# Up projections of the MLP: each 512-column product paired at once with its 256-column product, in place of eight and then eight

## The chip, the cores and the metric

The kernel runs on one core of a Trainium2 chip. The time of a run is the device time of that core in microseconds (us). The kernel before took 2586.78 us (median of three runs, 2585.1 to 2587.87).

## The reference

The program computes two layers of a hybrid encoder trunk over 256 tokens of width 2048, all in float32. Layer 0 has a Mamba-2 mixer, layer 1 an MLA attention mixer; each layer then has a squared-ReLU MLP and a gated per-layer input. The change touches the first product of the MLP, `hn @ w1`:

```python
D_MODEL = 2048; SEQ = 256; DEPTH = 2; D_FF = 4 * D_MODEL

def sq_relu_mlp(hn, w1, w2):
    return jnp.square(jax.nn.relu(hn @ w1)) @ w2

def reference(x, p, ...):
    h = x
    for i in range(DEPTH):
        hn = rmsnorm(h, ln_mix[i])
        h = h + (mamba2_mixer(hn, ...) if i < N_A else mla_mixer(hn, ...))
        h = h + sq_relu_mlp(rmsnorm(h, ln_mlp[i]), mlp_w1[i], mlp_w2[i])
        h = per_layer_input(h, p[i], ple_norm[i], ple_gate_w[i], ple_proj_w[i])
    return h
```

So for each of the two layers the up projection multiplies 256 x 2048 activations by a 2048 x 8192 matrix.

## The kernel before

Every float32 operand of a large matrix product is split into a high part and a rest ("hi" and "lo"), and the product is the sum hi x hi + hi x lo + lo x hi. Weights come from memory in slices of 2 x 128 rows by 512 columns (512 KB), through eight buffers `raw`. For each slice the scalar engine writes the high part to `w_hi` (line 647) and the vector engine the rest to `w_lo` (line 1197). Both have four slots, picked by `g % SPL`, where `g` counts slices. The semaphore "lo" says that a slice's rest is written; the semaphore "used", raised by the last product of a slice, gives its slot back to the scalar engine, which waits for it before it converts the slice four places further on.

TensorE works through the slices in a fixed order written in the program. Most projections are a `unit`: eight slices, each of 24 products of 512 columns (lines 1842 to 1844, in `half_chunk`), where the activations are the stationary operand and the weights stream.

The up projection, `up` inside `mlp`, is the other way round: the weights are stationary, in blocks of 128 x 128, and the activations stream. For one slice (this text calls that a round) there are four groups of output features (`f`) and two row tiles of the slice (`k`), which makes eight blocks. The high activations and their rest lie side by side in `xa_both`, 256 columns each, so that one product of 512 columns with a block of `w_hi` gives hi x hi in the first half of a bank of PSUM and hi x lo in the second (line 2083). A product of 256 columns with the block of `w_lo` then adds lo x hi into the first half (line 2089). Each `f` has a bank of its own (two in each of two pairs; the pairs are "acc_a" or "acc_b", "mid" and "tp" in the profile). Before, a round does the eight products of 512 columns for all four banks, then the eight of 256 columns. Every product has its own weight load just ahead of it.

Each `up(j)` is eight rounds, one for each slice of the 2048 rows, and each layer has 16 of them: four `up` in a row, 32 rounds, then units of the down projection. This makes 8 blocks of 32 rounds, 256 rounds in all. Between the first rounds of a layer's first block, jobs (`turn_h`) put eight transposes of `h` between two rounds: twice in layer 0 and once in layer 1. The round starts with a wait for "lo" (line 2076), and `hold` waits until a pair of banks has been read out, before the first product into it.

Of the kernel before, what the change touches and what calls it, by code (L numbers as in the profile page):

```python
# [105 lines left out]
def trunk_kernel(nc, x, p, positions, ln_mix, ln_mlp, mlp_w1, mlp_w2, ple_norm, ple_gate_w, ple_proj_w,  # L106
# [4 lines left out]
    with ctx:  # L111
# [36 lines left out]
        def part(*shape):  # L148
# [7 lines left out]
            if len(shape) == 3:  # L156
# [57 lines left out]
        halves = {"A": acc_a[:, :, :], "B": acc_b[:, :, :], "M": mid_both[:, :, :],  # L214
                  "T": tflat.rearrange("p (b n) -> p b n", b=2)}
# [1599 lines left out]
        def _(pe):  # L1815
            w = Walk(pe)

            def hold(banks, event):

                for b in banks:  # L1820
                    if b in w.busy:
                        name, k = w.busy[b]
                        pe.wait_ge(S[name], w.at(name, k))
                k = w.tick(event) + 1
                for b in banks:
                    w.busy[b] = event, k
# [22 lines left out]
            def chunk(*args):  # L1849

                for _ in half_chunk(*args):
                    pass
# [21 lines left out]
            def unit(x, pair, event, jobs=None, need=None):  # L1874


                hold(pair, event)
                for n in range(8):
                    if need and n % 2 == 0:
                        pe.wait_ge(S["act"], w.at("act", need[n // 2]))  # L1880
                    chunk(x, 2 * n, pair, n == 0, n == 7)
                    for job in (jobs or {}).get(n, ()):
                        job()

            def flip(src, per, n, m):

                for j in range(n):
                    for t in range(m):
                        last = pe.transpose(per(j, t), src(j, t), ident[:, :])  # L1889
                return last  # L1890
# [9 lines left out]
            def turn_h(blk, updates, scaled=True):  # L1900

                def job():
                    if updates:
                        pe.wait_ge(S["hadd"], updates)
                    if scaled:
                        hold_scaled()
                    else:
                        hold("T", "act")
                    flip(lambda j, t: h[:, t, 512 * blk + P * j:512 * blk + P * j + P], feature, 4, NT)\
                        .then_inc(S["Th"], 1)  # L1910
                return job
# [154 lines left out]
            def needs(posted):  # L2066

                return [w.k["act"] - posted + 1 + n for n in range(4)]

            def mlp(layer, pp, turns, posted):  # L2070
                def up(j, jobs=None, need=None):
                    for n in range(8):
                        if need and n % 2 == 0:
                            pe.wait_ge(S["act"], need[n // 2])
                        g = w.tick("G")
                        pe.wait_ge(S["lo"], g + 1)
                        for f in range(4):
                            half = (pp[0] + "M", "T" + pp[1])[j % 2][f // 2]
                            if n == 0 and f % 2 == 0:
                                hold(half, "u")  # L2080
                            dst = halves[half][:, f % 2]
                            for k in range(2):
                                pe.matmul(dst, w_hi[:, g % SPL, k, P * f:P * f + P],  # L2083
                                          xa_both[:, 2 * n + k].rearrange("p a t -> p (a t)"),
                                          start=n == 0 and k == 0, stop=False)
                        for f in range(4):
                            dst = halves[(pp[0] + "M", "T" + pp[1])[j % 2][f // 2]][:, f % 2]
                            for k in range(2):
                                mm = pe.matmul(dst[:, 0:TOK], w_lo[:, g % SPL, k, P * f:P * f + P],  # L2089
                                               xa_both[:, 2 * n + k, 0], start=False, stop=n == 7 and k == 1)  # L2090
                        mm.then_inc(S["used"], 1)
                        for job in (jobs or {}).get(n, ()):
                            job()

                def turn_p():
                    pe.wait_ge(S["pin"], 16 * (layer + 1))
                    hold("T", "act")
                    flip(lambda j, t: p_sb[:, t, P * j:P * j + P], feature, 2, NT).then_inc(S["Tp"], 1)

                base = 32 + 32 * layer + 12  # L2100
                up(0, turns, needs(posted))
                for q in range(4):
                    for j in range(1, 4):
                        up(j)
                    done = w.k["act"]
                    w.skip("act", 4)
                    unit(ya, pp[0], "hadd", None, range(done + 1, done + 5))
                    if q < 3:
                        for j in range(1, 4):
                            unit(ya, pp[j % 2], "hadd")  # L2110
                        up(0)
                unit(ya, pp[1], "hadd", {1: [turn_h(0, base + 1)]})
                unit(ya, pp[0], "hadd", {1: [turn_h(1, base + 2)], 4: [turn_p]})
                unit(ya, pp[1], "hadd", {1: [turn_h(2, base + 3)]})
                c = w.k["act"]
                pe.wait_ge(S["act"], c - 1)
                for n, pair in enumerate((pp[0], "M", pp[1], "M")):
                    hold(pair, "pj")
                    chunk(pt, 0, pair, True, True)
                    if n == 1:  # L2120
                        turn_h(3, base + 4)()
                jobs = lambda n, slot: {slot: [turn_h(n, base + 5 + n, scaled=False)]} if layer == 0 else {}
                unit(xa, pp[0], "gs", None, [c - 3, c - 2, c, c + 1])
                for n in range(2 + (layer == 0)):
                    unit(xa, pp[(n + 1) % 2], "gs", jobs(n, 3))
                if layer:
                    hold(pp[1], "gs")
                    for n in range(6):
                        chunk(xa, 2 * n, pp[1], n == 0, False)
                    g = w.k["G"]  # L2130
                    pe.wait_ge(S["lo"], g + 2)
                    for t, a, b in LAST_PIECES:
                        rows, dst = slice(t * P, t * P + P), acc[pp[1]][t][:, a:b]
                        for k in range(4):
                            xh, xl = xa[0][:, 12 + k, rows], xa[1][:, 12 + k, rows]
                            slot = (g + k // 2) % SPL
                            wh, wl = w_hi[:, slot, k % 2, a:b], w_lo[:, slot, k % 2, a:b]
                            pe.matmul(dst, xh, wh, start=False, stop=False)
                            pe.matmul(dst, xh, wl, start=False, stop=False)
                            mm = pe.matmul(dst, xl, wh, start=False, stop=k == 3)  # L2140
                        mm.then_inc(S["fin"], 1)
                w.skip("hadd", NB)
                return base
# [192 lines left out]
```

## Time and profile before

| | |
|---|---|
| runs before, median (lowest to highest) | 2586.78 us (2585.1 to 2587.87) |
| the profiled execution's own time | 2585.33 us |
| its span, first to last instruction | 2583.5 us |
| TensorE products busy | 2568.7 us, 99% of the span |
| TensorE weight loads busy | 2174.3 us, 84% |
| vector engine busy | 1657.0 us, 64% |
| scalar engine busy | 1262.2 us, 49% |
| GpSimd busy | 103.2 us, 4% |
| data read from memory | 486.38 MB, 189 GB/s over the span |
| granted TensorE clock | 1.000 of full speed |

All rows come from one profiled execution; its time lies 2585.33 - 2583.5 = 1.83 us over its span, for what comes before the first and after the last instruction. Products follow one another in a pipeline: the recorded duration of one (390 ns for one of 512 columns) is longer than the distance to the start of the next, so the cost of a product is read from the distance between starts in the list of instructions by time, not from its duration. In that list the first column is the start in us from the span's start, the second the time until the last instruction of the row ends, then the engine, line, operation, the output and inputs, and how many equal instructions one row stands for. "PE" are products, "PEld" weight loads. A product of 512 columns reads "128x512", one of 256 columns "128x256"; "128*128" is the block of weights (rows by columns).

### The profile page before, as it was taken

The numbers are of one execution on the slowest core, as the hardware profiler recorded it, in microseconds if no ns is written. First come the engines' busy times: TensorE is split into PE (matmuls) and PEld (weight loads), VectorE is DVE, ScalarE is ACT, GpSimd is POOL, SyncE is SP. The second block draws the span as 40 slices with busy tenths as digits, with TensorE's granted clock in tenths as the row PEclk, the third lists the DMA queues.
The fourth block names the chain that finished last, engine by engine and source line by source line (L and its number), as shares of the span: only waits on it lengthen the run. The fifth ranks groups of instructions, "written<-read, shape, count | busy, mean of one in ns | idle before, by whom it ended". The sixth has DMA issues, their size and how long they took to land.

```text
span 2583.5 us, 31623 instructions
## 1 busy us (share of the span) xinstructions
PE 2568.7 (99%) x12792; PEld 2174.3 (84%) x12792; DVE 1657.0 (64%) x1881; ACT 1262.2 (49%) x1528; POOL 103.2 (4%) x214
## 2 busy tenths in 40 slices
PE   9999999999999999999999999999999999999999
PEld 8888888888888888888888888888888888888887
DVE  6678888888755565555555567767655555555655
ACT  6545555555544443443445557655434434434453
POOL 2000000000000000000000002100000000000000
PEclk9999999999999999999999999999999999999999
DMA  7587887876565655656655554446556566566553
GB/s 258 156 280 242 235 240 240 240 224 203 175 193 194 189 190 193 189 193 193 190 192 180 189 170 134 144 157 180 190 192 189 193 193 189 189 194 188 192 187 130
DMA packets 263665, 503.11 MB, mean 195 GB/s; under 512 B 21840, under 2 KB 27208, under 8 KB 263520
## 3 DMA queue, kind: packets, MB, share of 16 engines
q1 hardware_dynamic: 259344, 490.88, 60.1%
q0 software_dynamic: 2656, 8.58, 1.2%
q8 instruction: 101, 1.65, 0.3%
q10 hardware_dynamic: 1520, 1.64, 0.2%
q14 instruction: 44, 0.36, 0.0%
HBM read 486.38 MB, written 2.16 MB: 189 GB/s over the span
## 4 chain that ended last, share of the span: by engine, by line
PE 95%; DVE 2%; DMA 1%; ACT 1%; issue 0%; POOL 0%; SPq 0%; ACTq 0%; DVEq 0%
PE acc_b L1842 10%; PE acc_b L1844 10%; PE acc_b L1843 10%; PE acc_a L1842 10%; PE acc_a L1844 10%; PE acc_a L1843 10%; PE tp L2083 5%; PE acc_b L2083 5%; PE acc_a L2083 5%; PE mid L2083 5%; PE mid L2089 2%; PE acc_b L2089 2%; PE acc_a L2089 2%; PE tp L2089 2%; PE tp L1889 2%; PE mid L2022 1%
## 5 line engine op out<-in xcount | busy, mean ns | idle before, releaser
L1197 DVE TENSOR_TENSOR w_lo<-raw,w_hi 128x1024 fp32r<-128x1024 f32 x874 | 1060.9, 1220 | 793.9 <-ACT w_hi L647 792.0
L647 ACT ACTIVATE w_hi<-raw 128x1024 fp32r<-128x1024 f32 x874 | 917.6, 1055 | 1081.0 <-PE acc_b L1844 344.2
L1842 PE MATMUL acc_b<-w_hi,ya_hi 128*128 128x512 f32 x736 | 288.8, 392 | 1.4 <-issue 1.4
L1844 PE MATMUL acc_b<-w_hi,ya_lo 128*128 128x512 f32 x736 | 286.7, 390 | 0.0
L1843 PE MATMUL acc_b<-w_lo,ya_hi 128*128 128x512 f32 x736 | 286.6, 389 | 0.0
L1842 PE MATMUL acc_a<-w_hi,ya_hi 128*128 128x512 f32 x704 | 276.0, 392 | 0.0
L1844 PE MATMUL acc_a<-w_hi,ya_lo 128*128 128x512 f32 x704 | 274.3, 390 | 0.0
L1843 PE MATMUL acc_a<-w_lo,ya_hi 128*128 128x512 f32 x704 | 274.1, 389 | 0.0
L1842 PE MATMUL acc_a<-w_hi,xa 128*128 128x512 f32 x512 | 202.2, 395 | 1.7 <-DVE w_lo L1197 1.7
L1844 PE MATMUL acc_a<-w_hi,xa 128*128 128x512 f32 x512 | 199.7, 390 | 0.0
L1843 PE MATMUL acc_a<-w_lo,xa 128*128 128x512 f32 x512 | 199.4, 390 | 0.0
L1842 PE MATMUL acc_b<-w_hi,xa 128*128 128x512 f32 (+1 forms) x472 | 183.0, 388 | 2.6 <-DVE w_lo L1197 2.5
L1844 PE MATMUL acc_b<-w_hi,xa 128*128 128x512 f32 (+1 forms) x472 | 180.5, 383 | 0.0
L1843 PE MATMUL acc_b<-w_lo,xa 128*128 128x512 f32 (+1 forms) x472 | 180.4, 382 | 0.0
L1842 PEld LDWEIGHTS acc_b<-w_hi,ya_hi 128*128 128x128 f32 x736 | 138.3, 188 | 29.6 <-issue 1.8
L1844 PEld LDWEIGHTS acc_b<-w_hi,ya_lo 128*128 128x128 f32 x736 | 138.1, 188 | 28.9
L1843 PEld LDWEIGHTS acc_b<-w_lo,ya_hi 128*128 128x128 f32 x736 | 138.3, 188 | 27.6
L1844 PEld LDWEIGHTS acc_a<-w_hi,ya_lo 128*128 128x128 f32 x704 | 132.2, 188 | 27.6
L1843 PEld LDWEIGHTS acc_a<-w_lo,ya_hi 128*128 128x128 f32 x704 | 132.3, 188 | 26.5
L1842 PEld LDWEIGHTS acc_a<-w_hi,ya_hi 128*128 128x128 f32 x704 | 132.2, 188 | 26.4
L2083 PE MATMUL tp<-xa,w_hi 128*128 128x512 f32 x512 | 139.9, 395 | 0.0
L2083 PE MATMUL acc_b<-xa,w_hi 128*128 128x512 f32 x512 | 138.7, 392 | 0.0
(341 smaller groups left out, 3487.7 us busy)
## 6 DMA issues: line engine op xcount, KB each, us to landing
raw<-in_mlp_w SPq DMA_DIRECT2D x512, 512.0 KB, 3.7
raw<-in_ssm_in_w SPq DMA_DIRECT2D x161, 512.0 KB, 6.0
raw<-in_ssm_out_w SPq DMA_DIRECT2D x64, 512.0 KB, 5.5
raw<-in_ple_gate_w SPq DMA_DIRECT2D x64, 512.0 KB, 3.7
raw<-in_mla_out_w SPq DMA_DIRECT2D x32, 512.0 KB, 3.6
rows<-in_ssm_conv_w SPq DMA_DIRECT2D x32, 256.0 KB, 5.8
scratch<-cumulative POOLq DMA_DIRECT2D x16, 512.0 KB, 7.5
raw<-in_ple_proj_w SPq DMA_DIRECT2D x8, 512.0 KB, 3.6
```

Of the source, the lines that this page charges most:

```text
L647: act.activation(w_hi[:, g % SPL, :, 0:cols], raw[:, g % RAW, :, 0:cols], ACT.Copy)\
L1197: dve.tensor_tensor(w_lo[:, g % SPL, :, 0:cols], raw[:, g % RAW, :, 0:cols], w_hi[:, g % SPL, :, 0:cols].bitcast(F32), ALU.subtract).then_ ...
L1842: pe.matmul(dst, xh, wh, start=first and k == 0, stop=False)
L1843: pe.matmul(dst, xh, wl, start=False, stop=False)
L1844: mm = pe.matmul(dst, xl, wh, start=False, stop=last and k == 1)
L1889: last = pe.transpose(per(j, t), src(j, t), ident[:, :])
L2022: last = pe.matmul(mid[b][:, HDIM * n:HDIM * n + HDIM], dec[b][:, n], xdt[:, b, n], start=True, stop=True)
L2083: pe.matmul(dst, w_hi[:, g % SPL, k, P * f:P * f + P], xa_both[:, 2 * n + k].rearrange("p a t -> p (a t)"), start=n == 0 and k == 0, stop= ...
L2089: mm = pe.matmul(dst[:, 0:TOK], w_lo[:, g % SPL, k, P * f:P * f + P], xa_both[:, 2 * n + k, 0], start=False, stop=n == 7 and k == 1)
```

## The change

In each round the product of 256 columns with the rest of a block now follows at once the product of 512 columns with the high part of the same block, on the same bank. The second pair of loops goes. The number of products, weight loads, waits and semaphore updates is the same; the last product of a round is the same one as before and raises "used" as before.

```diff
                         for f in range(4):
                             half = (pp[0] + "M", "T" + pp[1])[j % 2][f // 2]
                             if n == 0 and f % 2 == 0:
                                 hold(half, "u")
                             dst = halves[half][:, f % 2]
                             for k in range(2):
                                 pe.matmul(dst, w_hi[:, g % SPL, k, P * f:P * f + P],
                                           xa_both[:, 2 * n + k].rearrange("p a t -> p (a t)"),
                                           start=n == 0 and k == 0, stop=False)
-                        for f in range(4):
-                            dst = halves[(pp[0] + "M", "T" + pp[1])[j % 2][f // 2]][:, f % 2]
-                            for k in range(2):
                                 mm = pe.matmul(dst[:, 0:TOK], w_lo[:, g % SPL, k, P * f:P * f + P],
                                                xa_both[:, 2 * n + k, 0], start=False, stop=n == 7 and k == 1)
                         mm.then_inc(S["used"], 1)
```

TensorE's order at the start of the second block of rounds (L1844 is the last product of a down projection) is, before:

```order
L1844 MATMUL acc_a<-w_hi,ya_lo 128x512
L2083 MATMUL acc_b<-xa,w_hi 128x512 x4
L2083 MATMUL mid<-xa,w_hi 128x512 x4
L2089 MATMUL acc_b<-xa,w_lo 128x256 x4
L2089 MATMUL mid<-xa,w_lo 128x256 x4
L2083 MATMUL acc_b<-xa,w_hi 128x512 x4
```

The same place after the change (line 2086 is what line 2089 was):

```order
L1844 MATMUL acc_a<-w_hi,ya_lo 128x512
L2083 MATMUL acc_b<-xa,w_hi 128x512
L2086 MATMUL acc_b<-xa,w_lo 128x256
L2083 MATMUL acc_b<-xa,w_hi 128x512
L2086 MATMUL acc_b<-xa,w_lo 128x256
L2083 MATMUL acc_b<-xa,w_hi 128x512
L2086 MATMUL acc_b<-xa,w_lo 128x256
L2083 MATMUL acc_b<-xa,w_hi 128x512
L2086 MATMUL acc_b<-xa,w_lo 128x256
L2083 MATMUL mid<-xa,w_hi 128x512
```

Where a run of eight and a run of eight stood, the two kinds now alternate one by one: eight pairs in a round.

At the end of the first block, where a down projection takes over (L1842 to L1844), TensorE's order is, before:

```order
L2083 MATMUL acc_a<-xa,w_hi 128x512 x4
L2089 MATMUL tp<-xa,w_lo 128x256 x4
L2089 MATMUL acc_a<-xa,w_lo 128x256 x4
L1842 MATMUL acc_b<-w_hi,ya_hi 128x512
L1843 MATMUL acc_b<-w_lo,ya_hi 128x512
```

And after:

```order
L2083 MATMUL acc_a<-xa,w_hi 128x512
L2086 MATMUL acc_a<-xa,w_lo 128x256
L2083 MATMUL acc_a<-xa,w_hi 128x512
L2086 MATMUL acc_a<-xa,w_lo 128x256
L1842 MATMUL acc_b<-w_hi,ya_hi 128x512
L1843 MATMUL acc_b<-w_lo,ya_hi 128x512
```

The products of 512 columns of the down projection now come behind one product of 256 columns in place of eight. The order of the instructions on the scalar, the vector and the DMA-issuing engine is the same in both programs.

## Rows read from the trace of the kernel before

**Rows 1.** The profile's page: the span, busy time of each engine
```profile
span 2583.5 us, 31623 instructions
PE 2568.7 (99%) x12792; PEld 2174.3 (84%) x12792; DVE 1657.0 (64%) x1881; ACT 1262.2 (49%) x1528; POOL 103.2 (4%) x214
PE 95%; DVE 2%; DMA 1%; ACT 1%; issue 0%; POOL 0%; SPq 0%; ACTq 0%; DVEq 0%
```

**Rows 2.** Who waited for whom: us in total, times, longest wait in us
```profile
ACT w_hi L647 <- PE mid L2089: 193.4, 122, 1.7
...
PE acc_b L1842 <- DVE w_lo L1197: 2.5, 2, 1.6
```

**Rows 3.** Second block of 32 rounds, whole and without its first round
```profile
core 0: us, PE busy (x) PEld busy (x) DVE busy (x) ACT busy (x) POOL busy (x), PEclk, DMA share, GB/s
866.34:955.70 89.36, 89.36 (x514) 78.68 (x513) 50.96 (x46) 39.70 (x41) 0.00 (x0) 1.00 0.62 189
869.10:955.70 86.60, 86.60 (x499) 76.23 (x498) 49.55 (x45) 38.64 (x40) 0.00 (x0) 1.00 0.62 189
```

**Rows 4.** TensorE by time: first two rounds of the second block
```profile
866.11 0.39 PE L1844 MATMUL acc_a<-w_hi,ya_lo 128*128 128x512 f32 x1
866.34 1.07 PE L2083 MATMUL acc_b<-xa,w_hi 128*128 128x512 f32 x4
867.24 1.07 PE L2083 MATMUL mid<-xa,w_hi 128*128 128x512 f32 x4
868.15 0.64 PE L2089 MATMUL acc_b<-xa,w_lo 128*128 128x256 f32 x4
868.62 0.64 PE L2089 MATMUL mid<-xa,w_lo 128*128 128x256 f32 x4
869.10 1.09 PE L2083 MATMUL acc_b<-xa,w_hi 128*128 128x512 f32 x4
870.03 1.07 PE L2083 MATMUL mid<-xa,w_hi 128*128 128x512 f32 x4
870.94 0.64 PE L2089 MATMUL acc_b<-xa,w_lo 128*128 128x256 f32 x4
871.41 0.64 PE L2089 MATMUL mid<-xa,w_lo 128*128 128x256 f32 x4
871.89 0.40 PE L2083 MATMUL acc_b<-xa,w_hi 128*128 128x512 f32 x1
```

**Rows 5.** TensorE by time: the end of that block, then a down projection
```profile
955.70 0.40 PE L1842 MATMUL acc_b<-w_hi,ya_hi 128*128 128x512 f32 x1
...
956.86 0.39 PE L1844 MATMUL acc_b<-w_hi,ya_lo 128*128 128x512 f32 x1
```

**Rows 6.** TensorE by time: two places 24 products apart in a down projection
```profile
1000.60 0.39 PE L1842 MATMUL acc_b<-w_hi,ya_hi 128*128 128x512 f32 x1
...
1006.04 0.39 PE L1842 MATMUL acc_b<-w_hi,ya_hi 128*128 128x512 f32 x1
```

**Rows 7.** TensorE by time: 256 columns on weight blocks of 64 columns
```profile
35.34 0.28 PE L1861 MATMUL mid<-xa,w_lo 128*64 128x256 f32 x1
...
36.24 0.28 PE L1860 MATMUL mid<-xa,w_hi 128*64 128x256 f32 x1
```

**Rows 8.** Lines 2083 and 2089: durations in ns, least/median/most, of loads and products
```profile
L2083 PE MATMUL mid<-xa,w_hi x512: 388/389/395, 689.1 to 2365.7; 128*128 128x512 f32 x171
L2083 PE MATMUL tp<-xa,w_hi x512: 388/396/398, 712.2 to 2387.2; 128*128 128x512 f32 x171
...
L2089 PE MATMUL acc_b<-xa,w_lo x512: 277/283/284, 690.0 to 2389.1; 128*128 128x256 f32 x171
L2089 PEld LDWEIGHTS mid<-xa,w_lo x512: 191/192/193, 690.3 to 2366.7; 128*128 128x128 f32 x171
L2089 PE MATMUL mid<-xa,w_lo x512: 282/283/284, 690.4 to 2366.8; 128*128 128x256 f32 x171
```

**Rows 9.** TensorE by time: three transposes between products of 512 columns
```profile
1592.38 0.39 PE L1844 MATMUL acc_a<-w_hi,xa 128*128 128x512 f32 x1
1592.61 0.49 PE L2246 MATMUL tp<-ident,scratch 128*128 128x128 f32 x3
1592.86 0.48 PE L1842 MATMUL acc_a<-w_hi,xa 128*128 128x512 f32 x1
1593.17 0.39 PE L1843 MATMUL acc_a<-w_lo,xa 128*128 128x512 f32 x1
...
1594.10 0.40 PE L1844 MATMUL acc_a<-w_hi,xa 128*128 128x512 f32 x1
```

**Rows 10.** TensorE by time: four small products between products of 512 columns
```profile
218.32 0.40 PE L1844 MATMUL acc_b<-w_hi,ya_lo 128*128 128x512 f32 x1
...
219.44 0.39 PE L1843 MATMUL acc_b<-w_lo,ya_hi 128*128 128x512 f32 x1
...
220.35 0.39 PE L1844 MATMUL acc_b<-w_hi,ya_lo 128*128 128x512 f32 x1
```

## The prediction

> **What bounds the kernel now.** I read the page first: TensorE's products are busy for 2568.7 of 2583.5 us, and the chain that ended last is 95% TensorE [rows 1]. Then who waited for whom, to see whether TensorE waits for anything: of the waits of products the one of 2.5 us for `w_lo` is among the longest, while the scalar engine waits 193.4 us in 122 waits for one pair of banks of the up projection alone [rows 2]. So conversion has slack and TensorE sets the time. Then the stretch of one block of rounds: the granted clock is 1.00 and the DMA engines are 0.62 busy, the vector and scalar engine 51 and 40 of 89 us [rows 3]. Last, the list by time: a busy TensorE still hides how far apart its products start, and that distance is all that this change can touch.
>
> **The prices, from starts.** In a down projection 24 products of 512 columns take 1006.04 - 1000.60 = 5.44 us, 226.7 ns each [rows 6]. A product of 256 columns behind others of its kind takes (871.89 - 871.41) / 4 = 120 ns [rows 4]. Eight of each would be 8 x 0.2267 + 8 x 0.120 = 2.773 us.
>
> A round in the trace takes more: without its first round the block has 31 rounds in 86.60 us, 2.7935 us each [rows 3]. The surplus is 20.5 ns a round. Where is it? The first round of the block comes out of a long run of 512s and takes 2.76 us, the second 2.79 [rows 4]. Both have the same scalar and vector work beside them and the same instructions, so it is history that counts. Their first four 512s take 0.90 us in the first round and 0.93 in the second; the rest is nearly alike. The same happens to a down projection that follows a block: its first five 512s take 1.16 us, 232 ns each [rows 5]. I call these slow 512s the tail. So a run of eight 256s is paid for partly afterwards, in the 512s behind it.
>
> Inside there is a second, smaller thing. The first 256 behind a run of 512s is recorded with 277 ns, the others with 283, and the 512s of "tp", which come first in their rounds, with 396 ns in the median against 389 of "mid" [rows 8]. So the first product behind a change of kind is off by some 6.5 ns: the 256 cheaper, the 512 dearer. I read it as the weight load's share. 256 columns on a block of only 64 weight columns take (36.24 - 35.34) / 8 = 113 ns [rows 7] against 120 on 128 columns, so loading costs the stream about 7 ns per 64 columns. A load is recorded with 192 ns [rows 8], longer than a 256 lasts (120) and shorter than a 512 (227). Behind a 256 half of its cost falls into the next product; behind a 512 none does. That gives 113.3 for a 256 behind a 512, 233.3 for a 512 behind a 256, and their sum is again 346.7 ns. It cancels in each pair.
>
> The Trainium skill, "TensorE: Matmul & The Clock Gate", Part 2, says that PE has two independent read ports, so that loading the next weights takes nothing from the running matmul. By that alone the 64-column blocks would show no difference; rows 7 against rows 4 show about 7 ns, and the measurement decides.
>
> **The change, part by part.**
> 1. Removed, added: nothing. 16 products, 16 loads, the same waits and the same last product that raises "used". So the scalar engine gets its slot at the same point of a round, the vector engine and the DMA queue keep their order. Cost 0. If a round gets 20 ns shorter, they have to keep up; the scalar engine waits up to 1.7 us for TensorE in each of these waits [rows 2], so they can.
> 2. The second pair of banks is first written behind eight products in place of four, later, so the `hold` in front of it can only be easier. TensorE had no wait there worth a row. Gain 0.
> 3. On one bank a 256 now adds to what the 512 has just written, and the next 512 behind it. Two 256s on one bank one behind the other cost 120 ns before too [rows 4], a distance just as short. Cost 0.
> 4. The small step at a change of kind comes 16 times a round in place of twice, eight up and eight down. By the working above they cancel: 0.
> 5. The tail. Does it come behind one 256 as it does behind eight? There is no alternation of this kind in the trace, so I bound it. Behind three transposes (128 columns each) the tail is there: 4 products in 1594.10 - 1593.17 = 0.93 us, 232.5 ns [rows 9]. Behind four small products of another kind it is not: 4 in 220.35 - 219.44 = 0.91 us, 227.5 ns [rows 10]. The number of small products can't be the reason, since the four leave less than the three. The rate can. Each product is two instructions. Between the 512s, the three transposes take (1593.17 - 1592.38 - 2 x 0.2267) / 3 = 112 ns, 56 ns an instruction; the four take (219.44 - 218.32 - 2 x 0.2267) / 4 = 167 ns, 83 ns an instruction. A run of 256s has 60 ns an instruction. It looks as if TensorE's supply of instructions falls behind below some 60 to 80 ns and catches up during the next 512s. Alternating, a pair of 346.7 ns has four instructions, 87 ns each, on the side where no tail was seen. So I take no tail: 2.773 us a round.
>
> The sum: there are 256 runs of eight 256s. Three of them are followed by transposes, behind which the tail stays. 253 x 20.5 ns = 5.2 us less. Against the profiled execution, 2585.33 - 5.2 = 2580.1 us. This execution is 1.45 us below the median of the runs, so on the median's scale 2586.78 - 5.2 = 2581.6 us, -0.20%.
>
> Bounds for 5: the best is that a 256 always costs 113.3 and a 512 always 226.7, so 340 ns a pair, 2.720 us a round; a block of 89.36 us becomes 87.04, with the down projection's tail 2.34 us less, 8 x 2.34 = 18.7 us. The worst is the whole surplus of 20.5 ns at each of eight returns to a 512: 2.773 + 0.164 = 2.937 us, 256 x 0.1435 = 36.7 us more. I take the value nearest to rows 10.
>
> **The rivals.**
> - Larger gain: the dearer first 512 belongs to the tail and not to the load's share, and goes with it. Then the best bound holds: 2586.78 - 18.7 = 2568.1 us. For it: both appear at the same place. Against it: the step of the 256 and that of the 512 are of one size, 6 to 7 ns, as one load's share would be.
> - No change: the time of a round goes by its instructions and not by their order, 2586.8 us. The Trainium skill, "TensorE: Matmul & The Clock Gate", section "Back-to-back issue gap", gives each matmul N/2.4 plus a fixed 2.5 ns, which no order can alter. As a mechanism of this kernel: the surplus of 20.5 ns is the debt of eight 256s, 2.6 ns each, and is paid in whatever order. Rows 9 and 10 speak against it, weakly.
> - Slower: the tail never ends. It is set off by any short product and each 512 is the first behind one, so every 512 costs the 232.5 ns of rows 9, and the 256 its 120. The round is 8 x 352.5 = 2.820 us, 256 x 26.5 ns = 6.8 us more: 2593.6 us. It decides from the point where a pair costs over 2793.5 / 8 = 349.2 ns, only 2.5 ns over my value. For it: three transposes, 0.34 us, were enough for a full tail. Its extreme is the worst bound, 2623.5 us.
> - That the change doesn't do what it says: the order of instructions has the alternation in all rounds, so no chance is given.
>
> **How the numbers follow.** What a measurement of this kernel can tell from no change is about 0.2%, 5.2 us. The forecast gets 0.45, with 2579 to 2584 us for its own; it lies on the edge, so I count half as faster (0.22) and half as same (0.23). Larger gain 0.13, faster. No change 0.16, same. Slower 0.26, of which 0.03 for the extreme and 0.02 for a price so little over break-even that it reads as same. Faster 0.22 + 0.13 = 0.35, same 0.23 + 0.16 + 0.02 = 0.41, slower 0.24. The range goes from the larger gain to a little over the slower rival, 2568 to 2595 us, and leaves out the extreme and the outer parts of these two.
>
> **What would show it.** Rounds of 2.77 us in the list by time, the first of a block and the others alike. The 512s of line 2083 recorded with some 396 ns on all banks and the 256s with 277. Five 512s behind a block in 1.14 us in place of 1.16. Tail still there and rounds of 2.79 or 2.82 would say that one 256 is enough to set it off; 512s at 389 ns beside 256s at 277 and rounds of 2.72, that the larger gain is right. If TensorE shows waits for `w_lo` that it had not, step 1 was wrong.

## The result, and the profile after

The changed kernel takes 2593.33 us (median of 14 runs, 2590.41 to 2596.13), the kernel before, run beside it, 2587.78 us (14 runs, 2584.64 to 2590.15). The ratio is 1.0022, with a 95% interval of 1.0015 to 1.0029: slower by 5.5 us, where the prediction had 5.2 us faster as its likeliest case.

The page of the kernel after has the same numbers of instructions as before [rows 1] and a span that is 10.6 us longer (one profiled execution of each; the block times of this text come from one execution of each kernel too):

```profile
span 2594.1 us, 31623 instructions
PE 2577.1 (99%) x12792; PEld 2173.2 (84%) x12792; DVE 1656.5 (64%) x1881; ACT 1262.4 (49%) x1528; POOL 103.1 (4%) x214
```

Not all of the 10.6 us belongs to the change. The first up product starts at 693.2 us (688.2 before), which is ahead of all that was changed. Most of this lies in one stretch of the mixer, where this execution waits longer and then shows a lower granted clock. First after, then before, by stretch (us, busy and count of each engine, granted clock, DMA share, GB/s):

```profile
120.00:168.00 48.00, 44.02 (x181) 35.50 (x180) 32.84 (x50) 18.79 (x20) 4.74 (x8) 0.93 0.83 255
```
```profile
120.00:168.00 48.00, 46.14 (x202) 37.56 (x201) 34.93 (x53) 19.21 (x21) 4.75 (x8) 1.00 0.80 257
```

In it TensorE waits 2.89 us for the rest of a slice (`w_lo`), where it waited 1.62 us before. The granted clock falls before the longer wait ends and is 0.50 (1.2 GHz) from 160 to 166 us; before, it stays at 1.00 (2.4 GHz) in the same stretch. The code up to here is the same in both kernels.

What is left, 5.5 us, is in the eight blocks of rounds. Six of them look like the second, which took 89.36 us before [rows 3]; two have transposes among their first rounds, the first and the fifth (the first block of layer 1). The fifth before:

```profile
1769.75:1859.98 90.23, 90.23 (x521) 79.55 (x520) 55.05 (x50) 42.40 (x47) 1.80 (x6) 1.00 0.62 193
```

The second and the fifth after:

```profile
870.96:961.40 90.44, 90.44 (x513) 78.40 (x512) 50.94 (x46) 39.70 (x41) 0.00 (x0) 1.00 0.62 187
1777.63:1867.35 89.72, 89.72 (x521) 79.13 (x520) 54.99 (x50) 42.41 (x47) 1.75 (x6) 1.00 0.62 194
```

The second block is 1.08 us longer than before, the fifth 0.51 us shorter. The clock, the share of the DMA engines and the work of the vector and scalar engines are what they were. So the change made some blocks faster and others slower. The list by time shows the two paces. Here is the third block, with the time at which each product starts:

```profile
1100.04 0.40 PE L2083 MATMUL acc_b<-xa,w_hi 128*128 128x512 f32 x1
1100.28 0.28 PE L2086 MATMUL acc_b<-xa,w_lo 128*128 128x256 f32 x1
1100.40 0.40 PE L2083 MATMUL acc_b<-xa,w_hi 128*128 128x512 f32 x1
...
1101.10 0.40 PE L2083 MATMUL mid<-xa,w_hi 128*128 128x512 f32 x1
```

Three pairs take 1101.10 - 1100.04 = 1.06 us, 353.3 ns each; the first has 240 + 120 in the hundredths that the rows show. And the fifth block:

```profile
1799.75 0.39 PE L2083 MATMUL mid<-xa,w_hi 128*128 128x512 f32 x1
...
1800.79 0.39 PE L2083 MATMUL tp<-xa,w_hi 128*128 128x512 f32 x1
```

Three pairs in 1.04 us, 346.7 ns each, the price of the forecast. In a round that is 2.827 against 2.773 us, beside 2.7935 us before. The second block begins like this, behind the down projection:

```profile
870.96 0.39 PE L2083 MATMUL acc_b<-xa,w_hi 128*128 128x512 f32 x1
...
871.30 0.40 PE L2083 MATMUL acc_b<-xa,w_hi 128*128 128x512 f32 x1
...
871.65 0.40 PE L2083 MATMUL acc_b<-xa,w_hi 128*128 128x512 f32 x1
871.89 0.28 PE L2086 MATMUL acc_b<-xa,w_lo 128*128 128x256 f32 x1
```

The first pair takes 0.34 us, the second 0.35, and the third 512 is the first slow one (0.24 us). From there on the block keeps the slow pace. Blocks 1 and 5 start in the same way and change to the fast pace behind the transposes among their first rounds (in block 5 from the fourth round on).

Where the second block ends and the down projection takes over, the list has, behind a single product of 256 columns:

```profile
961.29 0.28 PE L2086 MATMUL acc_a<-xa,w_lo 128*128 128x256 f32 x1
961.40 0.40 PE L1842 MATMUL acc_b<-w_hi,ya_hi 128*128 128x512 f32 x1
...
962.56 0.39 PE L1844 MATMUL acc_b<-w_hi,ya_lo 128*128 128x512 f32 x1
```

The first five 512s take 1.16 us, as much as they took behind eight 256s [rows 5]; the prediction had 1.14. So the tail is there in full behind a block of pairs.

### The profile page after: what moved, and what is told of

Its sections match the earlier page's. It is cut to its first block, busy times and chain, and to the rows that moved or that the text cites. A ratio compares the mean times of both kernels' runs of the same rounds, so it can differ in the third digit from the quotient of the medians.

```text
span 2594.1 us, 31623 instructions
## 1 busy us (share of the span) xinstructions
PE 2577.1 (99%) x12792; PEld 2173.2 (84%) x12792; DVE 1656.5 (64%) x1881; ACT 1262.4 (49%) x1528; POOL 103.1 (4%) x214
## 4 chain that ended last, share of the span: by engine, by line
PE 95%; DVE 2%; DMA 1%; ACT 1%; issue 0%; POOL 0%; SPq 0%; ACTq 0%; DVEq 0%
PE acc_b L1842 10%; PE acc_b L1844 10%; PE acc_b L1843 10%; PE acc_a L1842 10%; PE acc_a L1844 10%; PE acc_a L1843 10%; PE mid L2083 5%; PE acc_a L2083 5%; PE acc_b L2083 5%; PE tp L2083 5%; PE acc_b L2086 2%; PE mid L2086 2%; PE acc_a L2086 2%; PE tp L2086 2%; PE tp L1889 2%; PE mid L2022 1%
## 5 line engine op out<-in xcount | busy, mean ns | idle before, releaser
L1842 PE MATMUL acc_b<-w_hi,ya_hi 128*128 128x512 f32 x736 | 288.8, 392 | 1.4 <-issue 1.4
L1844 PE MATMUL acc_b<-w_hi,ya_lo 128*128 128x512 f32 x736 | 286.6, 389 | 0.0
L1842 PE MATMUL acc_a<-w_hi,ya_hi 128*128 128x512 f32 x704 | 275.8, 392 | 0.0
L1844 PE MATMUL acc_a<-w_hi,ya_lo 128*128 128x512 f32 x704 | 274.1, 389 | 0.0
L1842 PE MATMUL acc_a<-w_hi,xa 128*128 128x512 f32 x512 | 202.1, 395 | 2.6 <-DVE w_lo L1197 2.6
L1844 PE MATMUL acc_a<-w_hi,xa 128*128 128x512 f32 x512 | 199.6, 390 | 0.0
L1842 PE MATMUL acc_b<-w_hi,xa 128*128 128x512 f32 (+1 forms) x472 | 184.0, 390 | 3.9 <-DVE w_lo L1197 3.8
L2083 PE MATMUL acc_b<-xa,w_hi 128*128 128x512 f32 x512 | 186.0, 397 | 0.0
L2083 PE MATMUL mid<-xa,w_hi 128*128 128x512 f32 x512 | 186.0, 397 | 0.0
L2083 PE MATMUL acc_a<-xa,w_hi 128*128 128x512 f32 x512 | 185.9, 397 | 0.0
L2083 PE MATMUL tp<-xa,w_hi 128*128 128x512 f32 x512 | 185.8, 397 | 0.0
L1844 PE MATMUL acc_b<-w_hi,xa 128*128 128x512 f32 (+1 forms) x472 | 181.5, 384 | 0.0
L1842 PEld LDWEIGHTS acc_b<-w_hi,ya_hi 128*128 128x128 f32 x736 | 138.2, 188 | 29.6 <-issue 1.8
L1844 PEld LDWEIGHTS acc_b<-w_hi,ya_lo 128*128 128x128 f32 x736 | 138.1, 188 | 29.1
L1844 PEld LDWEIGHTS acc_a<-w_hi,ya_lo 128*128 128x128 f32 x704 | 132.1, 188 | 27.6
```

Of the source, the lines that this page charges most:

```text
L1842: pe.matmul(dst, xh, wh, start=first and k == 0, stop=False)
L1844: mm = pe.matmul(dst, xl, wh, start=False, stop=last and k == 1)
L2083: pe.matmul(dst, w_hi[:, g % SPL, k, P * f:P * f + P], xa_both[:, 2 * n + k].rearrange("p a t -> p (a t)"), start=n == 0 and k == 0, stop= ...
```

## The experiments

Most runs change only the order of the products in a round. The third and the last leave out or change parts of the computation, for the time alone; the third and the sixth add waits to TensorE's stream. The two loops become one over a table of orders, and a function says which order a round has. "call" counts the four `up` of a block, `n` the eight rounds of one; blocks count from 0 in the code and from 1 in this text. "h" is the product of 512 columns, "l" the one of 256.

```diff
+EIGHT = [(f, k) for f in range(4) for k in range(2)]
+def grouped(size):
+    out = []
+    for a in range(0, 8, size):
+        out += [("h", f, k) for f, k in EIGHT[a:a + size]] + [("l", f, k) for f, k in EIGHT[a:a + size]]
+    return out
```

### Groups of eight, four, two and one

```diff
+    if block == 1: return "g4"
+    if block == 2: return "g2"
+    if block == 3: return "back" if n % 2 else "g8"    # back: eight l, then eight h
+    if block == 5: return "apart" if n else "g1"       # apart: l goes to bank f + 2
+    if block == 6: return "lead" if n else "g1"        # lead: l ahead of h
+    if block == 7: return "g1" if call or n else "g8"
+    return "g1" if block else "g8"
```

> Before, a round of the up projection took 2.7935 us (eight 512-column products, then eight of 256); after the change six of the eight blocks of 32 rounds ran at 2.8267 us a round (353.3 ns a pair) and the two blocks whose first rounds are broken up by transposes at 2.773 us (346.7 ns a pair). Here the blocks differ in the order of the products only. Block 1 and block 5 (counted from 1): eight and eight, and pairs. Block 2: four and four. Block 3: two and two. Block 4: eight and eight, with the order turned round in every second round, so that there is half as much going back from 256s to 512s. Block 6: pairs, but the 256-column product goes to a bank two places away. Block 7: pairs with the 256-column product ahead. Block 8: pairs, with eight and eight in the first round only. Theory 1, each return from 256s to 512s costs the same 20 ns, however few the 256s: 2.814 us a round in block 2, 2.855 in block 3, 2.783 in block 4 and blocks 6 to 8 like the slow pairs. Theory 2, alternation has two steady paces, and what ran just ahead picks one: block 8 at 2.773 in place of 2.827, since a run of 256s comes ahead as the transposes did. Theory 3, the slow pace comes from adding twice in a row to the same bank: block 6 at 2.773 or less, block 7 like the slow ones.

The stretches of blocks 2, 3, 4, 6, 7 and 8:

```profile
867.98:957.77 89.79, 89.79 (x514) 78.47 (x512) 50.95 (x46) 39.73 (x41) 0.00 (x0) 1.00 0.62 188
1044.86:1134.02 89.16, 89.16 (x514) 77.80 (x512) 50.93 (x46) 39.73 (x41) 0.00 (x0) 1.00 0.62 190
1221.07:1310.14 89.07, 89.07 (x514) 78.74 (x513) 50.93 (x46) 39.72 (x41) 0.00 (x0) 1.00 0.61 189
1948.12:2038.55 90.43, 90.43 (x513) 78.40 (x512) 50.94 (x46) 39.70 (x41) 0.00 (x0) 1.00 0.62 187
2125.62:2215.21 89.59, 89.59 (x514) 78.06 (x513) 50.93 (x46) 39.72 (x41) 0.00 (x0) 1.00 0.61 188
2302.27:2392.67 90.40, 90.40 (x514) 78.44 (x513) 50.94 (x46) 39.70 (x41) 0.00 (x0) 1.00 0.61 188
```

Divided by 32, with eight and eight at 89.36 / 32 = 2.793 us: four and four 2.806 (theory 1 had 2.814), two and two 2.786 (theory 1 had 2.855), turned round in every second round 2.783, as theory 1 had it. So with runs of eight one return from 256s to 512s costs about 20 ns, and half as many returns cost half; with shorter runs the price isn't fixed, and theory 1 falls. Sending the 256 to another bank changes nothing (90.43 us), which excludes theory 3. A first round of eight and eight does not help either (90.40 us): it isn't enough that short products stand ahead. With the 256 ahead the block runs partly at one pace and partly at the other, 89.59 us in all; it changes at the rounds of plain pairs that stand at the head of the second, third and fourth `up`.

### Other entries

```diff
+    first = not call and not n
+    if block == 1 and first: return "g8"
+    if block == 2 and first: return "g4"
+    if block == 3 and first: return "g2"
+    if block in (4, 7) and call == 2 and not n: return "g8"
+    if block == 5 and not call: return "g8"
+    if block == 6 and not call: return "g2"
+    return "g1"
```

> All blocks have pairs as after the change; only single rounds differ. Block 2 has eight and eight in its first round, block 3 four and four there, block 4 two and two there. Block 6 has eight and eight in its first eight rounds, block 7 two and two in its first eight. Blocks 5 and 8 have one round of eight and eight in the middle (round 17). Theory 2 (two steady paces, 2.773 and 2.827 us a round, picked by what ran just ahead): a block keeps its pace until the other round comes and can take the other one there; blocks 2 and 6 at 2.773 from their second or ninth round. Theory 1 (each return costs its 20 ns) and a theory that the pace belongs to the data or the place in memory: the odd rounds change nothing but themselves, and the pairs run at 2.827 all through.

Blocks 2, 3 and 4, whose first round is eight and eight, four and four, two and two:

```profile
867.94:958.33 90.39, 90.39 (x513) 78.41 (x512) 50.93 (x46) 39.70 (x41) 0.00 (x0) 1.00 0.62 187
1045.38:1134.14 88.76, 88.76 (x513) 78.25 (x512) 50.95 (x46) 39.73 (x41) 0.00 (x0) 1.00 0.62 190
1221.22:1309.97 88.75, 88.75 (x513) 77.61 (x512) 50.93 (x46) 39.75 (x41) 0.00 (x0) 1.00 0.62 190
```

One round in 32 decides over 1.6 us: 31 rounds of identical pairs take the fast pace behind four and four or two and two, the slow one behind eight and eight. The fifth block, fast behind its transposes, gets one round of eight and eight in its middle:

```profile
1771.15:1816.51 45.36, 45.36 (x266) 40.01 (x265) 28.47 (x26) 21.60 (x25) 1.75 (x6) 1.00 0.65 198
1819.30:1861.70 42.40, 42.40 (x242) 36.79 (x241) 25.10 (x23) 18.78 (x19) 0.00 (x0) 1.00 0.58 187
```

The 15 rounds behind it take 42.40 / 15 = 2.827 us each; fast ones would take 41.60. The odd round switched the pace off within one program, so the pace is no matter of data or place. Blocks 6 and 7 have eight rounds of eight and eight, and eight of two and two, at their head. Their other 24 rounds:

```profile
1971.10:2038.93 67.83, 67.83 (x387) 58.81 (x385) 39.82 (x36) 31.22 (x33) 0.00 (x0) 1.00 0.61 186
2148.28:2214.84 66.56, 66.56 (x387) 58.19 (x386) 39.81 (x36) 31.26 (x33) 0.00 (x0) 1.00 0.61 190
```

That is 2.826 us a round behind eight and eight and 2.773 behind two and two, as behind a single such round. The eighth block, slow from its start, stays slow behind its odd round. Theory 2 holds, but my idea of which round leads where did not: I had expected eight and eight to lead to the fast one.

The fast pace itself comes in two forms with the same mean. Behind four and four, and behind the transposes in the kernel after, each 512 is recorded with 391 ns and each 256 with 280. Behind two and two the records vary, 392 to 395 and 274 to 280. In the slow pace the 512s are recorded with 395 to 404 ns.

### What the second product reads, and how wide it is

```diff
+    return {1: "same", 2: "w384", 3: "w128", 5: "w8h", 6: "w8l", 7: "w1h"}.get(block, "g8")
```

> Parts of the computation are changed here, for the time alone: in block 2 the product of 256 columns takes its weights from the high part again, in blocks 3 and 4 the second product of a pair has 384 and 128 columns in place of 256. Blocks 2 to 4 are pairs. In block 6 the order is eight and eight with a wait (on a semaphore that is long since up) ahead of each 512, in block 7 the same ahead of each 256, in block 8 pairs with such a wait ahead of each 512. Blocks 1 and 5 are eight and eight. If the address of the weights matters, block 2 leaves 2.827 us; if not, it stays. Widths: 8 x (226.7 + 120 + 53.3) = 3.200 us a round is the plain sum for 384 columns, 8 x (226.7 + 66.7) = 2.347 for 128 columns, or 2.68 if a product can't be under 109 ns; a surplus over these like that of 256 says that any change of width costs. Theory 4, TensorE's supply of instructions falls behind in a run of short products and the slow 512s behind it are the catching up: extra instructions lengthen it, block 6 and 7 over 2.7935 us, block 7 more; block 8 slower than 2.827. If supply isn't it, blocks 6 and 7 stay at 2.79.

Blocks 2 (weights of the high part again), 3 (384 columns) and 4 (128 columns):

```profile
868.32:958.76 90.44, 90.44 (x514) 78.48 (x512) 50.94 (x46) 39.71 (x41) 0.00 (x0) 1.00 0.61 187
1045.82:1149.92 104.10, 104.10 (x514) 92.81 (x512) 50.91 (x46) 39.68 (x41) 0.00 (x0) 1.00 0.53 162
1236.97:1323.96 86.99, 86.99 (x514) 76.59 (x512) 50.92 (x46) 39.66 (x41) 0.00 (x0) 1.00 0.63 194
```

The address of the weights doesn't matter. With 384 columns a round is 3.25 us, 0.05 over the plain sum. With 128 columns it is 2.72 us, 340 ns a pair, and nowhere near the 293 ns of the plain sum: 340 - 226.7 leaves 113 ns for a product that streams half of what a 256 does. Halving the columns of a 256 makes a pair only 7 to 13 ns shorter. So with full weight blocks something other than the stream keeps a pair at 340 ns, and a pair with a 256 sits just above it. The waits in blocks 6 to 8 changed nothing, but most of them turned out to be attached to the products and not to be instructions of their own (the page has 31687 instructions, 64 more than before, for 768 waits), so they say little on theory 4. That is what the supply run below is for.

### Pairs with a chosen entry, first try

```diff
+    if block % 4 == 0 and not call and n < 3:
+        return "g8"
+    return "g2" if not call and n == (0 if block % 4 else 3) else "g1"
```

> Pairs everywhere as after the change, except at the entry of each block: its first round is two and two. In blocks 1 and 5, which transposes break up in their first three rounds, rounds 1 to 3 are eight and eight and round 4 is two and two. Theory 2 (alternation has two steady paces and what ran just ahead picks one; a first round of two and two led to 2.773 us a round in the one-look run): all blocks at 2.773 from the next round on. Six blocks of 88.75 us against 89.36 before, two with 28 rounds each 20 ns shorter: 6 x 0.61 + 2 x 0.56 = 4.8 us faster than before, 0.18 to 0.19%, and some 10 us faster than the changed kernel. A theory that pairs are slower in themselves, and the fast blocks were chance: like the changed kernel, 5 to 6 us slower than before.

The ratio to the kernel before is 0.9988, interval 0.9979 to 0.9996. Block 5:

```profile
1767.12:1858.28 91.16, 91.16 (x521) 79.27 (x520) 55.04 (x50) 42.40 (x47) 1.80 (x6) 1.00 0.62 191
```

Seven blocks are fast (88.75 us in the six behind a down projection), the fifth is slow. There the round of two and two stood behind a round of eight and eight; in the first block, with the same table, it stood directly behind transposes. So not the last round alone counts, but what stood ahead of that too.

### Two and two everywhere

```diff
+    return "g2"
```

> Two and two in all rounds (two products of 512 columns, then two of 256 for the same blocks). One block of it took 89.163 us against 89.36 before, with one pace. By the trace 8 x 0.197 = 1.6 us faster than before, 0.06%. If each return from 256s to 512s cost 20 ns (theory 1) it would be 256 x 61 ns = 15.7 us slower.

The ratio is 0.9992, interval 0.9983 to 1.0001: as forecast, too small to be told from no change by the times. In the trace the six blocks behind a down projection have 89.16 us each. Here are the last 29 rounds of the fifth, behind the transposes:

```profile
1778.50:1859.31 80.81, 80.81 (x467) 70.51 (x465) 48.15 (x43) 37.11 (x39) 0.00 (x0) 1.00 0.62 189
```

That is 2.786 us a round in the six and 2.787 here. So this order has one pace behind either of the two; behind other rounds it wasn't run for long.

### More instructions for TensorE

```diff
+                            if kind[0] == "w":
+                                for name, count in (("setup", 1), ("vt", 1), ("mix", 16)):
+                                    pe.wait_ge(S[name], count)
```

> One extra instruction (a wait on semaphores long since up, of a kind that stands as an instruction of its own in TensorE's stream) ahead of single products. Blocks 1 and 5: eight and eight as before. Block 2: eight and eight, extra instruction ahead of each 512. Block 3: eight and eight, ahead of each 256. Block 4: pairs, ahead of each 512. Block 6: pairs, ahead of each 256. Blocks 7 and 8: pairs, with the one extra instruction in rounds 1 and 17 alone (ahead of the first 512 in block 7, of the first 256 in block 8). Theory 4 (the slow 512s are TensorE's supply of instructions catching up): block 3 has three instructions in 120 ns, so its 256s get slower than 120 ns or its slow 512s last longer, and a round is clearly over 2.7935 us; block 2 is over it too; blocks 4 and 6 over 2.827. Rival: the surplus arises behind the supply, in the array's own sequence of loads and products; extra waits then cost nothing in themselves, blocks 2 and 3 stay at 2.79 and at most the pace of pairs flips to 2.773 where one disturbs the sequence (blocks 4, 6, 7, 8).

Blocks 3 (eight and eight; block 2 has 89.36 us as well) and 4 (pairs):

```profile
1045.89:1135.25 89.36, 89.36 (x513) 78.66 (x512) 50.95 (x46) 39.71 (x41) 0.00 (x0) 1.00 0.62 189
1222.32:1312.76 90.44, 90.44 (x514) 78.43 (x512) 50.94 (x46) 39.70 (x41) 0.00 (x0) 1.00 0.62 187
```

To the hundredth of a microsecond nothing moved, with three instructions for each product of 120 ns. Blocks 6, 7 and 8 have 90.44 us as well, so no pace changed either. Theory 4, on which step 5 of the prediction rested, is excluded in the form in which it was written down, that more instructions lengthen the tail.

### Pairs with a chosen entry, second try

```diff
+    entry = 0 if block % 4 else 2 if block else 3
+    if call or n > entry: return "g1"
+    return "g2" if n == entry else "g8"
```

> Pairs with a chosen entry: the first round of blocks 2 to 4 and 6 to 8 is two and two, behind the 512s of a down projection; in blocks 1 and 5 the two-and-two round stands directly behind the last transposes (round 4 and round 3), with eight and eight ahead of it. Theory 2: all eight blocks at 2.773 us a round behind the entry. Six blocks of 88.75 us and two that are 0.55 us shorter than before: 6 x 0.61 + 2 x 0.55 = 4.8 us under before, a ratio of 0.998, and 1.4 us under the run in which block 5 fell into the slow pace (91.16 us). Rival: the pace isn't set by what stands ahead of it in the program; then block 5 may be slow again.

2580.27 us (median of 11 runs) against 2585.86 us for the kernel before, run beside it; the ratio is 0.9982, interval 0.9973 to 0.9991. Block 5 (block 2 has 88.75 us again):

```profile
1767.44:1857.09 89.65, 89.65 (x522) 78.54 (x521) 55.02 (x50) 42.42 (x47) 1.80 (x6) 1.00 0.62 194
```

All eight blocks are at the fast pace. It is faster than the kernel before by 5.6 us, about what the prediction had forecast for the change alone, and so faster than the kernel after too.

### Entries of every length

```diff
+    size = {1: 2, 2: 3, 3: 4, 5: 5, 6: 6, 7: 7}.get(block)
+    if size and not call and not n: return "in%d" % size    # size h, size l, then pairs
+    return "g1"
```

> Pairs, but the first round of a block begins with a run of a 512s and then a 256s, and goes on in pairs: a = 2 in block 2, 3 in block 3, 4 in block 4, 5 in block 6, 6 in block 7, 7 in block 8. A run of eight led to 2.8267 us a round, four and four twice to 2.773, two and two four times to 2.773. Theory 2 in the form that only the length of the last run of 256s counts: one border, 2.773 below it and 2.827 above. Theory 2 in the form that the sequence of loads and products goes through a small set of states: the pace jumps between the two values without order in a. In either form no block has a third value. Rival (the pace drifts or is chance): other values, or a change inside a block.

All six are slow; the one with 7 at the entry takes 90.40 us, the one with 2

```profile
868.84:959.28 90.44, 90.44 (x513) 78.48 (x512) 50.95 (x46) 39.70 (x41) 0.00 (x0) 1.00 0.61 187
```

The two forms that I had written down are both wrong in their wording: there is neither a border nor a jumping about, since one run of 256s of any length from 2 to 7 behind 512s led to the slow pace. Rounds made of several short groups (four and four twice, two and two four times) led to the fast one; eight rounds of eight and eight did not. It would be handy to say that a second run of 512s has to be cut short by 256s while it is still slow from the first; but the fifth block of the first try above had that too, behind eight and eight, and was slow. No block has a third pace, and none changes inside.

### Narrow weight blocks

```diff
-                                mm = pe.matmul(dst, w_hi[:, g % SPL, k, P * f:P * f + P],
+                                mm = pe.matmul(dst[0:width], w_hi[:, g % SPL, k, P * f:P * f + width],
```

> In rounds 2 to 7 of each eight, some products use weight blocks of 64 columns in place of 128 and so leave out half of the outputs; this is for the time alone. Block 2: eight and eight, all narrow. Block 3: pairs, all narrow. Block 4: eight and eight, the 256s narrow. Block 6: eight and eight, the 512s narrow. Block 7: pairs, the 256s narrow. Block 8: pairs, the 512s narrow. Theory 5, the surplus over 8 x (226.7 + 120) ns comes from weight loads that last longer than a 256 and run into the next product: with all loads narrow the small step, the tail and the slow pace go, 8 x (220 + 113.3) = 2.667 us a round in blocks 2 and 3 alike. Rival, the surplus comes from the change of the number of columns streamed, whatever is loaded: block 2 keeps its 20 ns over the sum of its prices, and block 3 has one of two paces, 53 ns apart.

A round of eight and eight with all blocks narrow:

```profile
875.13 1.08 PE L2131 MATMUL acc_b<-xa,w_hi 128*64 128x512 f32 x4
...
876.97 0.63 PE L2135 MATMUL acc_b<-xa,w_lo 128*64 128x256 f32 x4
...
877.89 0.39 PE L2131 MATMUL acc_b<-xa,w_hi 128*64 128x512 f32 x1
```

2.76 us. The 256s are at 115 ns each (0.92 us for eight), near the 113 that 7 ns for 64 columns of load says. The 512s aren't at 220 ns: they take 1.84 us for eight, 230 ns, and so still have their tail. Pairs in which only the block of the 512 is narrow, which is the load that runs while a 256 streams:

```profile
2305.29 0.39 PE L2131 MATMUL acc_a<-xa,w_hi 128*64 128x512 f32 x1
...
2305.97 0.39 PE L2131 MATMUL mid<-xa,w_hi 128*64 128x512 f32 x1
```

Two pairs in 0.68 us, 340 ns, although each of these narrow stretches came out of wide rounds at the slow pace. Block 3, with all blocks narrow, has 340 ns too. Block 7 has the other load narrow, the one that runs while a 512 streams:

```profile
2129.89 0.39 PE L2131 MATMUL mid<-xa,w_hi 128*128 128x512 f32 x1
...
2130.93 0.39 PE L2131 MATMUL mid<-xa,w_hi 128*128 128x512 f32 x1
```

Three pairs in 1.04 us, 346.7 ns, again out of wide rounds at the slow pace, and the next wide rounds are slow again. So with either block narrow the slow pace was gone as long as the narrow blocks lasted, and what is left over 340 ns, 6.7 ns, goes when the load under a 256 is narrow. Theory 5 is right for pairs in this sense: their surplus hangs on full weight blocks. A narrow block shortens the load, but it also leaves its product only half of the output rows, and no run parts the two. The theory is wrong for the tail behind a long run, which stays: 2.76 us is 40 ns over eight pairs of 340 ns.

## Why the prediction was wrong

**The bound was right, and so was the price of a pair, in part by luck.** TensorE sets the time, nothing else moved, and the pair at its fast pace costs 346.7 ns as forecast. Its split is another: the forecast wanted 512s recorded with 396 ns and 256s with 277, and the fifth block has 391 and 280 in its fast rounds. Steps 1 to 3 hold: in the eight blocks there is no new wait on TensorE, and the run with the 256 on another bank shows that adding to the same bank costs nothing.

**The step that failed is step 5,** "So I take no tail: 2.773 us a round." It holds in two blocks of eight. The other six ran at 2.827 us a round, 33 ns over the round before where I had 20.5 under it. The sum: six blocks x 1.08 us = 6.5 us more, 0.46 us less in the first (90.65 against 91.11 us) and 0.51 us less in the fifth, together 5.5 us more. And the tail, which the step took to be absent where 256s stand singly, is there: five 512s take 1.16 us behind the last pair of a block, as behind eight 256s.

The argument for this step was the supply of instructions, 56 ns an instruction in rows 9 against 83 in rows 10. The second figure is a mean over two kinds, as the lines between those of rows 10 show:

```profile
218.56 0.60 PE L2011 MATMUL tp<-scratch 128*128 128x256 f32 x2
218.99 0.38 PE L2012 MATMUL tp<-scratch 128*128 128x128 f32 x2
```

The first two take 0.43 us, 215 ns each. The last two, ahead of the 512s without a tail, take (219.44 - 218.99 - 0.2267) / 2 = 112 ns each, the 112 ns of the transposes in rows 9, behind which there is a tail. So just ahead of the 512s the rate is the same in both places, and the mean of 167 ns can't carry the step. The number of such products, which the prediction had ruled out as the reason, is two against three and isn't excluded by these rows. With half as many instructions again in a run of 256s, all of them waits, the times are the same to 0.01 us.

**Step 4 was right in its sum and wrong in its rule.** Pairs do have a surplus that goes with narrow blocks. But it doesn't simply cancel: two paces are possible, 346.7 and 353.3 ns a pair, and a block of pairs keeps the one that it enters. Narrow blocks did not bring a 512 under 226.7 ns either, where the expectation of the last run had 220.

**The rival "slower"** had the right size, 352.5 ns a pair against 353.3 measured and 2593.6 us against 2593.33, for a reason that is half right: the 512s in the slow pace are dearer than in a plain run, at 230 to 240 ns by their starts. It was also right that 256s which stand singly leave a tail. It had the dear 512s everywhere, where two blocks are fast, and it took the tail for their cause. With narrow blocks pairs lose their surplus and a run of eight keeps it, which speaks for two different things. I had given it 0.26, and the measured ratio, 1.0022, is at the edge of what I had called slower, as the forecast was at the edge of faster.

**What stays open** is why the array has two paces, and by what rule an entry picks one. I can name entries that led to either, not a rule that gives them. The tail behind long runs is measured (20 ns a return, halved with half the returns) and not explained. How much of the supply a wait takes up beside a product isn't measured.

The Trainium skill, "TensorE: Matmul & The Clock Gate", section "LDWEIGHTS (loading the stationary operand)", gives a load the time of its columns at 1.2 GHz, 107 ns for 128. That stands close to the 113 ns that the pair of 340 ns leaves beside a 512. No run here shows the 107 itself: a load of 128 columns is recorded with 187 to 192 ns. The Trainium skill, "TensorE: Matmul & The Clock Gate", section "Back-to-back issue gap", gives the fixed 2.5 ns, on which the rival "no change" drew, for an isolated matmul, and says that in a stream of loads and matmuls both set the distance. That the order can't alter the time is not borne out here: 31 rounds of the same pairs differ by 1.6 us with the one round ahead of them.

## What to carry to other kernels

Where products of two lengths alternate, each with its own weight load, look at the distance between starts over many products, and expect it to depend on what ran before: a steady stretch can have two paces. Before taking a gain or a loss of 0.2% for that of the order itself, look at whether all stretches have the same pace, and whether one round put ahead of them switches it. The safe order is one that showed a single pace in all places where it was run (here two and two), the fastest one has to be entered rightly and checked in the trace block by block.

## What the runs showed of the hardware

- The same alternation of 512- and 256-column products runs at 346.7 or at 353.3 ns a pair in the mean, steadily for 15 to 32 rounds. The choice is made by the products ahead of it, and repeats in every block in which the same products stand there.
- A pair of a 512 and a product of 128 columns takes 340 ns, no less than a pair of a 512 and a 256 with narrow weight blocks.
- Behind a block of pairs, with a single 256 ahead, the first five 512s take 1.16 us, as much as behind eight 256s, against 1.13 us at the 226.7 ns of a long run.
- Extra wait instructions in TensorE's stream, one for each product of 120 ns, cost nothing: 89.36 us a block with and without them.
- One execution lost some 5 us in the mixer: it waited 2.89 us for `w_lo` where another waited 1.62, and its granted clock was 0.50 from 160 to 166 us. The runs of the kernel before spread by as much (5.5 us), and a difference of two single profiles has to be taken apart by stretch before it is given to a change.
